# Differential attention's projection blocks as fp32 matmuls straight from the ring, with a scaled copy of the input made on GpSimd, and two weight splits moved ahead of a VectorE wait

## The chip, the core and the metric

The kernel runs on one core of a Trainium2 chip. TensorE (PE) does the matmuls, VectorE (DVE), ScalarE (ACT) and GpSimd (POOL) the elementwise work, and SyncE's queue (SP) issues most of the DMAs. The metric is the time of one execution in microseconds (us) on the device; lower is better.

## The reference

A trunk of two layers over 256 tokens of width 1024, all in fp32. Each layer projects the normalised input, mixes with two parallel groups of heads (an RWKV-7 recurrence, and differential attention), then does cross-attention and a feed-forward part (dense in layer 0, top-2 of 8 experts in layer 1). Cut to the part that the change touches:

```python
for l in range(DEPTH):
    h = rms_norm(x, mix_norm[l])                       # x / rms(x) * gain
    w_in = in_proj[l] if l == 0 else concat([in_proj[l], vres_down[l - 1]])
    proj = h @ w_in                                    # 1792 + 1536 (+ 32) columns
    p_rwkv = token_shift(proj[..., :RWKV_COLS], shift_mu[l])   # p + (prev - p) * mu
    p_diff = proj[..., RWKV_COLS:IN_COLS]              # q, k, v of differential attention
    y_rwkv, v_l = rwkv7_time_mix(p_rwkv, ...)
    y_diff = diff_attention(p_diff, ...)
    x = x + concat([y_rwkv, y_diff]) @ out_proj[l]
    ...
```

## The kernel before

The 256 tokens are two tiles of 128 (`t`), the width is eight tiles of 128 (`k`). Weights come from memory in blocks of 512 KB (two `k` by 512 columns), into a ring of four slots (`ring`), fetched by SP in the order of the list `blocks`.

**Most blocks are split.** TensorE multiplies in the format fp32r. To keep the accuracy of fp32 each weight block is split into a high part, made by ScalarE (`hi_of`, L405 where a gain is multiplied in), and the rest, made by VectorE (`lo_of`, L419: `ring*gain - w_hi`, two instructions of 128x512 for a block). The input is split the same way into `h_hi` and `h_lo`. `product` (L465, L466, L467) then takes three matmuls for each pair of tiles. There are three slots for split blocks (`NS`). A ring slot is given free by VectorE's half of the split, a split slot by TensorE's use.

**Some blocks are direct.** The cross-attention's `wkv` blocks are multiplied in fp32 straight from the ring (L530, the stationary operand is `mem_T`); such a matmul stands in the trace as two records. TensorE's use gives the ring slot free.

**The input projection** of a layer has 28 blocks of which the first 16 are for the recurrence, four blocks to a group of columns: keys (blocks 0 to 3), the low-rank columns (4 to 7, half as wide), receptance (8 to 11), values (12 to 15). Blocks 16 to 27 (`inb`, generator `rest`) are the 1536 columns of differential attention. Block numbers below count from the layer's first. The rms scale is applied when a result is evacuated; the gain `mix_norm` is in the split weights. ScalarE evacuates a group (L1257), GpSimd issues three DMAs that shift it by one token (`shift_in`, L1184 to L1186), and VectorE mixes (`mix`: a subtraction, a product with `mu`, a sum).

**Order.** Each engine has one program written out by hand. VectorE calls `split_to(n)` between its steps to do all splits up to block n. It starts the keys' mix (`next(k_mix)`, which waits for the shifted key columns) after block 7, and does blocks 8, 9 and 10 between the steps of the mixes. From the mixed keys it makes `NB[KK]` (L1683); ScalarE squares them (L1287), VectorE sums (L1541) and scales. TensorE's order is: the 16 first blocks with small products between them, the cumulative sums (L629), four blocks of `rest`, a small product (L639), four blocks of `rest`, the transposes of `aT`, `rT`, `bT`, `kT` (L489; they wait for VectorE's `elem`), and then the recurrence, between whose steps stand the last four blocks of `rest`, some cut into halves (one half for each `t`).

**GpSimd** in layer 1 alone forms the sum of `h_hi` and `h_lo` into `hT` (L1208, four instructions of 128x512), for a small product with `vresd_w` (32 columns), whose gain VectorE multiplies into the weights.

## Time and profile before

| | |
|---|---|
| median of 3 runs | 1944.86 us (the lowest is 1944.83; one run of 10261.35 stands beside them) |
| the profiled execution | 1950.51 us, of which the span of the core is 1948.7 us |
| mean granted TensorE clock | 0.972 |
| busy share of the span | PE 94%, DVE 78%, ACT 62%, POOL 3% |
| layer 0's input projection and recurrence | about 0 to 250 us of the span |
| layer 1's | about 555 to 810 us |
| the experts | about 940 us to the end |

The page's busy shares are means over stages that differ. The matmuls are pipelined and their ends modelled, so the spacing of their starts tells more than their durations. A row of a timeline has the start, the busy time, the engine, the line, the operation with its output and inputs, and in brackets how long the engine stood idle before it and what ended that. The granted clock is a share of full speed, and has two levels (1.2 and 2.4 GHz).

### The profile page before, as it was taken

How to read it: one execution, taken by the hardware profiler on the slowest of the kernel's cores; microseconds unless marked ns; L12 is line 12 of the kernel's file. 1: busy time of each engine (PE TensorE's matmuls, PEld its weight loads, DVE VectorE, ACT ScalarE, POOL GpSimd, SP SyncE). 2: the span in 40 equal slices, each digit the busy share in tenths (PEclk: the TensorE clock that was granted, in tenths of full speed). 3: DMA queues.
4: the chain of work that ended last, by engine and by line, in shares of the span. 5: the costliest groups of instructions: out<-in, count | busy, mean ns of one | idle time of the engine just before them, and what ended most of it. 6: DMA issues, size and time to landing. Idle time of an engine off the chain costs nothing.

```text
span 1948.7 us, 31880 instructions
## 1 busy us (share of the span) xinstructions
PE 1832.7 (94%) x10685; PEld 1452.9 (75%) x10685; DVE 1523.9 (78%) x2106; ACT 1198.5 (62%) x1616; POOL 54.1 (3%) x90
## 2 busy tenths in 40 slices
PE   6988898999999887998899999999999999999998
PEld 5665566788876665577788888888888888888886
DVE  5874666655568765674799999999999999999997
ACT  4632444555555312552677888778877878878785
POOL 2000000000020000000300000000000000000000
PEclk9999899999999897999899999999999999999999
DMA  8521163466654311451799999999999999999994
GB/s 255 177 89 56 55 211 98 150 188 187 190 165 142 119 45 34 132 170 61 280 372 341 359 379 336 358 359 345 379 337 361 356 352 370 338 366 347 358 371 152
DMA packets 224014, 474.54 MB, mean 244 GB/s; under 512 B 16680, under 2 KB 41400, under 8 KB 223376
## 3 DMA queue, kind: packets, MB, share of 16 engines
q1 hardware_dynamic: 219456, 458.29, 66.8%
q0 software_dynamic: 3472, 13.65, 2.2%
q8 instruction: 56, 0.92, 0.2%
q10 hardware_dynamic: 960, 1.10, 0.2%
q14 instruction: 70, 0.57, 0.1%
HBM read 468.25 MB, written 1.05 MB: 241 GB/s over the span
## 4 chain that ended last, share of the span: by engine, by line
PE 82%; DVE 11%; ACT 3%; DMA 2%; issue 2%; POOL 0%; DVEq 0%; ACTq 0%; POOLq 0%
PE psum L465 22%; PE psum L467 22%; PE psum L466 22%; PE psum L530 4%; PE psum L489 3%; DVE w_lo L419 2%; PE psum L1002 2%; PE psum L1049 1%; DMA SH<-proj 1%; DVE SH L1561 1%; PE psum L893 1%; DVE NB L1532 1%; DVE st L1538 1%; ACT hN L1261 1%; DVE SH L1532 1%
## 5 line engine op out<-in xcount | busy, mean ns | idle before, releaser
L465 PE MATMUL psum<-w_hi,h_hi 128*128 128x512 f32 (+1 forms) x1648 | 653.7, 397 | 31.5 <-DVE w_lo L419 29.5
L467 PE MATMUL psum<-w_hi,h_lo 128*128 128x512 f32 (+1 forms) x1648 | 644.3, 391 | 0.0
L466 PE MATMUL psum<-w_lo,h_hi 128*128 128x512 f32 (+1 forms) x1648 | 644.0, 391 | 0.0
L465 PEld LDWEIGHTS psum<-w_hi,h_hi 128*128 128x128 f32 x1648 | 312.6, 190 | 106.1 <-DVE w_lo L419 27.0
L467 PEld LDWEIGHTS psum<-w_hi,h_lo 128*128 128x128 f32 x1648 | 312.3, 189 | 66.5
L466 PEld LDWEIGHTS psum<-w_lo,h_hi 128*128 128x128 f32 x1648 | 312.9, 190 | 62.7 <-issue 0.5
L419 DVE SCALAR_TENSOR_TENSOR w_lo<-ring,col,w_hi 128x512 fp32r<-128x512 f32 (+1 forms) x232 | 163.4, 750 | 75.2 <-ACT w_hi L405 73.6
L405 ACT ACTIVATE w_hi<-ring,col 128x512 fp32r<-128x512 f32 (+1 forms) x232 | 150.6, 701 | 114.3 <-PE psum L467 109.6
L435 DVE TENSOR_TENSOR w_lo<-ring,w_hi 128x1024 fp32r<-128x1024 f32 x144 | 172.2, 1220 | 7.7 <-ACT w_hi L431 3.2
L431 ACT ACTIVATE w_hi<-ring 128x1024 fp32r<-128x1024 f32 x144 | 151.9, 1060 | 41.1 <-PE psum L467 41.1
L435 DVE TENSOR_TENSOR w_lo<-dproj,w_hi 128x1024 fp32r<-128x1024 f32 x120 | 145.8, 1222 | 17.1 <-ACT w_hi L431 13.0
L431 ACT ACTIVATE w_hi<-dproj 128x1024 fp32r<-128x1024 f32 x120 | 127.8, 1065 | 36.1 <-PE psum L467 36.1
L435 DVE TENSOR_TENSOR w_lo<-SH,w_hi 128x1024 fp32r<-128x1024 f32 x120 | 143.8, 1220 | 6.3 <-ACT w_hi L431 4.1
L431 ACT ACTIVATE w_hi<-SH 128x1024 fp32r<-128x1024 f32 x120 | 127.7, 1064 | 23.3 <-PE psum L467 22.9
L465 PE MATMUL psum<-h_hi 128*128 128x512 f32 x336 | 137.1, 408 | 0.1
L467 PE MATMUL psum<-h_hi,h_lo 128*128 128x512 f32 x336 | 131.6, 392 | 0.0
L466 PE MATMUL psum<-h_lo,h_hi 128*128 128x512 f32 x336 | 131.1, 390 | 0.0
L530 PE MATMUL psum<-ring,mem_T 128*128 128x512 f32 x256 | 123.0, 622 | 0.0
L435 DVE TENSOR_TENSOR w_lo<-proj,w_hi 128x1024 fp32r<-128x1024 f32 x96 | 115.2, 1220 | 6.9 <-ACT w_hi L431 5.1
L414 DVE TENSOR_TENSOR w_lo<-ring,w_hi 128x1024 fp32r<-128x1024 f32 x54 | 65.7, 1224 | 68.6 <-ACT w_hi L400 68.5
L400 ACT ACTIVATE w_hi<-ring 128x1024 fp32r<-128x1024 f32 x54 | 57.2, 1060 | 93.0 <-PE psum L467 78.4
L431 ACT ACTIVATE w_hi<-proj 128x1024 fp32r<-128x1024 f32 x96 | 101.3, 1064 | 19.0 <-PE psum L467 19.0
(315 smaller groups left out, 2336.0 us busy)
## 6 DMA issues: line engine op xcount, KB each, us to landing
ring<-in_expert_w_gu SPq DMA_DIRECT2D x128, 512.0 KB, 5.4
SH<-in_expert_w_gu SPq DMA_DIRECT2D x120, 512.0 KB, 5.8
proj<-in_expert_w_gu SPq DMA_DIRECT2D x104, 512.0 KB, 6.1
dproj<-in_expert_w_gu SPq DMA_DIRECT2D x72, 512.0 KB, 5.8
dproj<-in_expert_w_down SPq DMA_DIRECT2D x72, 512.0 KB, 5.0
ring<-in_expert_w_down SPq DMA_DIRECT2D x64, 512.0 KB, 5.1
ring<-in_in_proj SPq DMA_DIRECT2D x48, 512.0 KB, 4.4
ring<-in_dense_w_gu SPq DMA_DIRECT2D x88, 256.0 KB, 3.1
```

What stands on the lines that cost most here:

```text
L400: ins = act.activation(w_hi[:, i % NS, :], ring[:, n % RING, :], ACT.Copy)
L405: ins = act.activation(hi[:, k, :], src[:, k, :], ACT.Copy, scale=col[:, l, a + k:a + k + 1])
L414: ins = dve.tensor_tensor(w_lo[:, i % NS, :], ring[:, n % RING, :], w_hi[:, i % NS, :].bitcast(F32), SUB)
L419: ins = dve.scalar_tensor_tensor(lo[:, k, :], src[:, k, :], col[:, l, a + k:a + k + 1], hi[:, k, :].bitcast(F32), MUL, SUB)
L431: act.activation(hi_e[j % NS_E], ring_e[j % RING_E], ACT.Copy).then_inc(hi_done, 1)
L435: dve.tensor_tensor(lo_e[j % NS_E], ring_e[j % RING_E], hi_e[j % NS_E].bitcast(F32), SUB).then_inc(lo_done, 1)
L465: pe.matmul(o, h[0], w[0], start=start, stop=False, skip_group_check=True)
L466: pe.matmul(o, h[0], w[1], start=False, stop=False, skip_group_check=True)
L467: return pe.matmul(o, h[1], w[0], start=False, stop=stop, skip_group_check=True)
L489: last = pe.transpose(bank[0:m, i * P:i * P + n], s, ident[0:n, 0:n])
L530: last = pe.matmul(banks[c][t][:, 0:cw], memT[:, kb + k, t * P:(t + 1) * P], wd[:, k, :], start=(kb + k == 0), stop=(kb + k == 7), skip_gr ...
L1002: last = pe.matmul(bank[:, k * P:(k + 1) * P], hNv[:, t, (4 * g + k) * P:(4 * g + k + 1) * P], Psel[:, t, :], start=(t == 0), stop=(t == 1))
```

## The change

1. The 12 `inb` blocks of each layer become direct: no split, and TensorE multiplies in fp32 from the ring.
2. A direct block has no gain in it, so GpSimd makes the input with the gain, `xg = (h_hi + h_lo) * gain`, in two new buffers (`gained_x`): twelve instructions for a layer, six sums and six products, each product waiting for its sum. Eight of the twelve are 128x256, four 128x512. In layer 1 they stand where the four sums stood; in layer 0, where there was nothing, between the issue of the low-rank columns' shift and that of the receptance columns.
3. TensorE waits for them (`raw_ready`) ahead of `rest`. The small product with `vresd_w` uses the new buffers too, and VectorE's product of `vresd_w` with the gain goes.
4. VectorE does the splits of blocks 8 and 9 ahead of its wait for the shifted keys, 10 and 11 between the steps of the keys' mix; ScalarE does its half of block 11 ahead of the squares.

```diff
+        xg_b = nc.alloc_sbuf_tensor_at("xg_b", [P, 512], F32, offset=h_base + 4 * 2048)
+        xg_a = sb("xg_a", [P, 1536])
...
-            blocks += square_blocks(in_proj[l], chunks_in[0:4], gain=(l, COL["mix"])) + square_blocks(in_proj[l], chunks_in[4:], gain=(l, COL["mix"]))
+            blocks += square_blocks(in_proj[l], chunks_in[0:4], gain=(l, COL["mix"]))
+            blocks += [("direct", src, cw, None) for _, src, cw, _ in square_blocks(in_proj[l], chunks_in[4:])]
...
-                            if src[0] == "mT":
-                                last = pe.matmul(banks[c][t][:, 0:cw], memT[:, kb + k, t * P:(t + 1) * P], wd[:, k, :],
+                            if straight:
+                                lhs = memT[:, kb + k, t * P:(t + 1) * P] if src[0] == "mT" else x_gained(kb + k, t)
+                                last = pe.matmul(banks[c][t][:, 0:cw], lhs, wd[:, k, :],
                                                  start=(kb + k == 0), stop=(kb + k == 7), skip_group_check=True)
...
-                    pe.wait_ge(raw_ready, 4)
-                    pe.wait_ge(side_ready, 1)
+                    pe.wait_ge(raw_ready, 2 * 8)
+                    pe.wait_ge(lw_in, 80)
...
-                            last = pe.matmul(bank[:, 0:VR], hTv[:, k, t * P:(t + 1) * P], vresd_w[:, k, :], start=(k == 0), stop=(k == 7))
+                            last = pe.matmul(bank[:, 0:VR], x_gained(k, t), vresd_w[:, k, :], start=(k == 0), stop=(k == 7))
...
+                pe.wait_ge(raw_ready, 8 * (l + 1))
                 some(rest, 4)
...
+            def gained_x(l):
+
+                gain = col[:, l, COL["mix"]:COL["mix"] + KD]
+                if l == 0:
+                    pool.wait_ge(col_in, 16)
+                n = 8 * l
+                for g in range(2):
+                    for t in range(TT):
+                        B.wait_evacuated(pool, ("hT", l, 0, t, g))
+                        for k0, kn in ((0, 4),) if g == 0 else ((4, 2), (6, 2)):
+                            to = xgs[k0 // 6][:, k0 % 6:k0 % 6 + kn, t * P:(t + 1) * P]
+                            of = [m[:, k0 * SEQ:(k0 + kn) * SEQ].rearrange("p (k t) -> p k t", t=SEQ)[:, :, t * P:(t + 1) * P] for m in (h_hi, h_lo)]
+                            step(pool.tensor_tensor(to, of[0].bitcast(F32), of[1].bitcast(F32), ADD))
+                            n += 1 if kn == 2 else 2
+                            pool.tensor_tensor(to, to, bc(gain[:, k0:k0 + kn].unsqueeze(2), kn, P), MUL).then_inc(raw_ready, 1 if kn == 2 else 2)
+                pool.wait_ge(raw_ready, n)
...
                 if l:
-                    for g in range(2):
-                        for t in range(TT):
-                            B.wait_evacuated(pool, ("hT", l, 0, t, g))
-                            pool.tensor_tensor(part(hT, g, t), part(h_hi, g, t).bitcast(F32), part(h_lo, g, t).bitcast(F32), ADD).then_inc(raw_ready, 1)
+                    gained_x(l)
...
                 shift_in(l, LORA_)
+                if l == 0:
+                    gained_x(l)
...
-                        split_to(base + 11)
+                        split_to(base + 12)
...
-                    tt(vresd_w[:, :, :], vresd_w[:, :, :], bc(gains(l, "mix").unsqueeze(2), KD, VR), MUL)
...
+                split_to(base + 10)
                 next(k_mix)
-                split_to(base + 9)
+                split_to(base + 11)
                 next(k_mix)
-                split_to(base + 10)
+                split_to(base + 12)
                 for m in [lora_mix] + ([vr_mix] if l else []):
                     next(m)
                     next(m)
-                split_to(base + 11)
```

VectorE in layer 0 before the change, from the keys' mix to the squares' sum: `SH` holds the shifted columns and `hN` is `mu`, `shifted_in0` is the keys' shift, `weights_hi` ScalarE's half of a split.

```order
L1532 TENSOR_TENSOR SH<-SH,proj 128x2x512 [waits shifted_in0,mu_in]
L419 SCALAR_TENSOR_TENSOR w_lo<-ring,col,w_hi 128x512 [waits weights_hi,dve_step]
L419 SCALAR_TENSOR_TENSOR w_lo<-ring,col,w_hi 128x512
L1532 TENSOR_TENSOR SH<-SH,hN 128x2x512
L1667 TENSOR_TENSOR proj<-proj,SH 128x2x512 [waits dve_step]
L419 SCALAR_TENSOR_TENSOR w_lo<-ring,col,w_hi 128x512 [waits weights_hi,dve_step]
L419 SCALAR_TENSOR_TENSOR w_lo<-ring,col,w_hi 128x512
```

The same place on VectorE after the change:

```order
L426 SCALAR_TENSOR_TENSOR w_lo<-ring,col,w_hi 128x512 [waits weights_hi,mu_in]
L426 SCALAR_TENSOR_TENSOR w_lo<-ring,col,w_hi 128x512
L426 SCALAR_TENSOR_TENSOR w_lo<-ring,col,w_hi 128x512 [waits weights_hi]
L426 SCALAR_TENSOR_TENSOR w_lo<-ring,col,w_hi 128x512
L1558 TENSOR_TENSOR SH<-SH,proj 128x2x512 [waits shifted_in0]
L426 SCALAR_TENSOR_TENSOR w_lo<-ring,col,w_hi 128x512 [waits weights_hi,dve_step]
L426 SCALAR_TENSOR_TENSOR w_lo<-ring,col,w_hi 128x512
L1558 TENSOR_TENSOR SH<-SH,hN 128x2x512
L1692 TENSOR_TENSOR proj<-proj,SH 128x2x512 [waits dve_step]
L426 SCALAR_TENSOR_TENSOR w_lo<-ring,col,w_hi 128x512 [waits weights_hi,dve_step]
L426 SCALAR_TENSOR_TENSOR w_lo<-ring,col,w_hi 128x512
```

Two splits (blocks 8 and 9) now stand ahead of the wait for `shifted_in0`, and each later one is two blocks further on, so that the split of block 11 no longer stands behind the squares.

GpSimd in layer 0 after the change, from the last DMA of the low-rank columns' shift on (before, the rows L1186 and L1184 followed each other here):

```order
L1196 DMA SH<-proj 1x16x16
L1210 ISA
L1210 TENSOR_TENSOR xg_a<-h_hi,h_lo 128x4x128 [waits psum_evacuated4,columns_in]
L1212 TENSOR_TENSOR xg_a<-xg_a,col 128x4x128 [waits pool_step]
L1210 TENSOR_TENSOR xg_a<-h_hi,h_lo 128x4x128 [waits psum_evacuated5]
L1212 TENSOR_TENSOR xg_a<-xg_a,col 128x4x128 [waits pool_step]
L1210 TENSOR_TENSOR xg_a<-h_hi,h_lo 128x2x128 [waits psum_evacuated6]
L1212 TENSOR_TENSOR xg_a<-xg_a,col 128x2x128 [waits pool_step]
```

Six more rows of 128x2x128 follow before the receptance columns' shift (L1194).

TensorE in layer 0 before the change, at the start of `rest`: the first of eight blocks, of twelve matmuls each, of which six are shown.

```order
L465 MATMUL psum<-w_hi,h_hi 128x512 [waits weights_lo,psum_evacuated1,psum_evacuated0]
L466 MATMUL psum<-w_lo,h_hi 128x512
L467 MATMUL psum<-w_hi,h_lo 128x512
L465 MATMUL psum<-w_hi,h_hi 128x512
L466 MATMUL psum<-w_lo,h_hi 128x512
L467 MATMUL psum<-w_hi,h_lo 128x512
```

The same place after it, four whole blocks of four matmuls:

```order
L539 MATMUL psum<-ring,xg_a 128x512 [waits psum_evacuated1,block_in0,psum_evacuated0,raw_xT_ready]
L539 MATMUL psum<-ring,xg_a 128x512 x3
L539 MATMUL psum<-ring,xg_a 128x512 [waits block_in1]
L539 MATMUL psum<-ring,xg_a 128x512 x3
L539 MATMUL psum<-ring,xg_a 128x512 [waits block_in2]
L539 MATMUL psum<-ring,xg_a 128x512 x3
L539 MATMUL psum<-ring,xg_b 128x512 [waits block_in3]
L539 MATMUL psum<-ring,xg_b 128x512 x3
```

The wait for VectorE's split (`weights_lo`) is gone there; the block's arrival (`block_in`) and GpSimd's buffers (`raw_xT_ready`) are waited for.

## Rows read from the trace of the kernel before

**Rows 1.** The page, part 4: the whole span's chain, by engine.

```profile
PE 82%; DVE 11%; ACT 3%; DMA 2%; issue 2%; POOL 0%; DVEq 0%; ACTq 0%; POOLq 0%
```

**Rows 2.** Layer 0, VectorE's timeline: start us, us, engine, line, operation, [idle before <-releaser].

```profile
34.11 1.23 DVE L1532 TENSOR_TENSOR SH<-SH,proj 128x1024 f32<-128x1024 f32 x1 [6.26 <-DMA SH<-proj]
...
43.28 1.41 DVE L419 SCALAR_TENSOR_TENSOR w_lo<-ring,col,w_hi 128x512 fp32r<-128x512 f32 x2
44.61 1.22 DVE L1683 TENSOR_TENSOR NB<-proj,vec 128x1024 f32<-128x1024 f32 x1
48.18 1.41 DVE L419 SCALAR_TENSOR_TENSOR w_lo<-ring,col,w_hi 128x512 fp32r<-128x512 f32 x2 [2.35 <-ACT w_hi L405]
49.51 1.21 DVE L1541 TENSOR_REDUCE st<-NB 128x16 f32<-128x1024 f32 x1
50.76 1.42 DVE L419 SCALAR_TENSOR_TENSOR w_lo<-ring,col,w_hi 128x512 fp32r<-128x512 f32 x2
```

**Rows 3.** Layer 0, timelines of ScalarE and then TensorE, same columns.

```profile
45.86 1.06 ACT L1287 ACTIVATE NB<-NB 128x1024 f32<-128x1024 f32 x1 [10.56 <-DVE NB L1683]
46.83 3.77 ACT L405 ACTIVATE w_hi<-ring,col 128x512 fp32r<-128x512 f32 x6
...
36.93 0.77 PE L465 MATMUL psum<-w_hi,h_hi 128*128 128x512 f32 x1 [6.69 <-DVE w_lo L419]
```

**Rows 4.** GpSimd's timeline, layer 0: issue of the receptance columns' shift.

```profile
54.00 0.68 POOL L1184 DMA_DIRECT2D SH<-proj  x1 [18.84 <-ACT proj L1257]
```

**Rows 5.** Layer 1: GpSimd's sums, VectorE's splits 558 to 569 us; ns, min/median/max.

```profile
L1208 POOL TENSOR_TENSOR hT<-h_hi,h_lo x4: 1252/1268/1737, 560.4 to 566.7; 128x512 f32<-128x512 f32 x4
...
L419 DVE SCALAR_TENSOR_TENSOR w_lo<-ring,col,w_hi x6: 739/1070/4067, 558.7 to 567.2; 128x512 fp32r<-128x512 f32 x6
```

**Rows 6.** GpSimd's timeline in the experts' part: small operations.

```profile
945.27 1.10 POOL L1238 TENSOR_TENSOR NB<-NB 128x4 f32<-128x4 f32 x1
...
950.20 0.19 POOL L1241 TENSOR_TENSOR NB<-NB 128x1 f32<-128x1 f32 x1
```

**Rows 7.** VectorE's timeline there.

```profile
945.09 1.22 DVE L435 TENSOR_TENSOR w_lo<-ring,w_hi 128x1024 fp32r<-128x1024 f32 x1 [0.24 <-DVE hT L2118]
...
949.66 1.27 DVE L2136 TENSOR_TENSOR y_lo<-psum,y_hi 128x512 fp32r<-128x512 f32 x2
```

**Rows 8.** The chain of waits, an fp32 block and half block: start, us.

```profile
712.96 3.44 PE psum L530 x8
...
731.28 1.91 PE psum L530 x4
```

**Rows 9.** TensorE by stretch: us, busy (x), granted clock, DMA share, GB/s.

```profile
75.29:86.28 10.99, 10.99 (x51) 1.00 0.49 146
87.98:100.39 12.41, 11.46 (x51) 1.00 0.53 159
624.24:635.55 11.31, 11.31 (x50) 1.00 0.59 177
637.25:656.08 18.83, 14.34 (x51) 0.82 0.55 163
667.00:672.00 5.00, 5.00 (x42) 0.73 0.00 0
```

**Rows 10.** VectorE's timeline, layer 0: first and last of four splits.

```profile
79.89 1.41 DVE L419 SCALAR_TENSOR_TENSOR w_lo<-ring,col,w_hi 128x512 fp32r<-128x512 f32 x2
...
93.19 1.41 DVE L419 SCALAR_TENSOR_TENSOR w_lo<-ring,col,w_hi 128x512 fp32r<-128x512 f32 x2
```

**Rows 11.** Layer 1, timelines of TensorE and VectorE: waits behind splits.

```profile
650.79 0.79 PE L465 MATMUL psum<-w_hi,h_hi 128*128 128x512 f32 x1 [3.57 <-DVE w_lo L419]
...
673.62 0.75 DVE L419 SCALAR_TENSOR_TENSOR w_lo<-ring,col,w_hi 128x512 fp32r<-128x512 f32 x1 [0.68 <-ACT w_hi L405]
```

**Rows 12.** Layer 1, VectorE, then ScalarE: after the row scale, and key columns.

```profile
571.23 1.67 DVE L419 SCALAR_TENSOR_TENSOR w_lo<-ring,col,w_hi 128x256 fp32r<-128x256 f32 x4
...
573.55 0.69 ACT L1257 ACTIVATE proj<-psum,st 128x512 f32<-128x512 f32 x1 [0.61 <-PE psum L467]
```

More of the change, by code:

```diff
@@ L219, in decoder_trunk, with x_gained @@
         memT = mem_T[:, :].rearrange("p (k t) -> p k t", k=KD)
+        xgs = [m[:, :].rearrange("p (k t) -> p k t", t=SEQ) for m in (xg_a, xg_b)]
+        def x_gained(k, t):
+            return xgs[k // 6][:, k % 6, t * P:(t + 1) * P]
         mu = hN[:, 0:NMU]
@@ L520, in project_steps @@
                             nproj[0] += 1
-                    if src[0] == "mT":
+                    straight = src[0] == "mT" or name[0] == "inb"
+                    if straight:
                         wd = take_direct(cw)
```

2 lines of the change are left out of this document (1 added, 1 removed).

## The prediction

> **What bounds the kernel now.** I read the page's chain first, then the chain of waits in time for the two stretches that hold the input projection and the recurrence, then the timelines of VectorE, ScalarE, GpSimd and TensorE there. The chain is TensorE's for most of the span [rows 1], and over half of the span is the experts' loop, whose instructions the change leaves as they are. So only the two layers' stretches can move, and there three things take turns.
>
> From the shift of the keys to the low-rank products the chain is VectorE's and ScalarE's. In layer 0 VectorE waits for the shifted keys until 34.11 and then works nearly without a gap to the scaled keys at 44.61. The split of block 10 stands ahead of them (43.28), and that of block 11 (48.18, after 2.35 us idle) ahead of the squares' sum at 49.51 [rows 2]: ScalarE makes its half of block 11 only after the squares of 45.86 [rows 3]. TensorE waits 6.69 us for the split of block 8, which stands behind the shifted keys [rows 3], but that wait does not end last.
>
> The second thing is `rest`. In layer 0 the first eight blocks take TensorE from 75.29 to 100.39, back to back but for a small product and 0.95 us; the clock is full. In layer 1 they take from 624.24 to 656.08 [rows 9], with a wait of 3.57 us for a split and then half the clock (0.82 over that stretch) [rows 9, 11]: there VectorE binds.
>
> The third is the recurrence, where the last four blocks fill TensorE between short steps.
>
> **A block in fp32 against a split block.** Four split blocks take 10.99 us at full clock [rows 9], 2.75 for one. A direct block of the same shape takes 3.44, and its half 1.91 with the start [rows 8]. That is +0.69 for a block, +8.3 for the twelve of a layer, wherever TensorE is what ends last. VectorE is relieved of 12 x 1.41 = 16.9 us and ScalarE of 12 x 1.26 = 15.1 in each layer [rows 2, 3]; this counts only where they end last.
>
> *Layer 0, `rest`:* eight blocks now 8 x 3.44 = 27.5, and the small product between the two fours, 86.28 to 87.98, 1.7: 29.2 in place of 25.1 [rows 9], **+4.1**. VectorE's inputs to the next step do not bind: its last split ended at 94.6, and four of them (79.89 to 93.19) go [rows 10], so it is ready 5.6 us earlier, some 15 us before TensorE gets there.
>
> *Layer 1, `rest`:* 29.2 in place of 31.84 [rows 9], **-2.6**, since the wait and the half clock after it go.
>
> *The last four blocks, in the recurrence:* 4 x 0.69 = 2.8 if TensorE bound all through, nothing if the waits for the other engines cover it. In layer 0 I take **+1.5**, the middle, since the first of them already hides ScalarE's copies. In layer 1 the clock is 0.73 from 667 to 672 [rows 9], so one block takes about 4.1, and a pair of split instructions behind 0.68 us of waiting (673.62) stands on the chain [rows 11]; these go, up to 2.2. I take **-0.7**, between -2.2 and +2.8.
>
> The blocks' arrival adds no wait that I can find: a slot is now freed by TensorE's use, but four blocks lie ready when `rest` begins, and the DMA share is about a half there [rows 9].
>
> **The moved splits.** In layer 0, left alone, the scaled keys come 1.3 us earlier (block 10's split is no longer between) and end at 44.5; the squares follow at once, 1.06, and the sum starts at about 45.8 in place of 49.51 [rows 2, 3]: **-3.7** for all that follows (block 12's split, the scale, block 13, the low-rank products, the values and their shift). In layer 1 I take **-2.4**: VectorE then meets block 10 sooner than ScalarE's half of it is made, one such half (1.26) [rows 3]. Neither end can be on the plus side here, since no instruction is added.
>
> **The buffers made by GpSimd.** This is the term that decides. A sum of 128x512 takes 1.25 [rows 5], a tiny operation 0.19 [rows 6], so one of 128x256 about 0.72 (estimate, midway). The product with a stretched gain has no row; its nearest is the sum, and I take the same. Four of 1.25 and eight of 0.72 make 10.8 us for a layer. In layer 0 GpSimd stands idle from 35.16 to 54.00, 18.84 us [rows 4], so its own queue has room: the receptance shift behind it is late only if that work stretches past 54.
>
> But does VectorE go on meanwhile? In layer 1 now, four sums run between 560.4 and 568.3, and the splits of VectorE, 0.74 us at best, have a median of 1.07 and one of 4.07 [rows 5]. In the experts' part a GpSimd operation on four elements takes 1.10 beside a split that reads two tiles from SBUF, and 0.19 beside VectorE's operations that read PSUM [rows 6, 7]. So the two engines shut each other out for whole instructions. The Trainium skill says the same in "SBUF — State Buffer", section "SBUF: two separate sides": the shared port pair is an exclusive lock for the whole instruction, taken by a VectorE operation with two SBUF inputs only against a GpSimd one that reads SBUF. By that rule it speaks against this change, and the trace agrees.
>
> *Layer 0:* from 35.2 VectorE has ten instructions with two SBUF inputs up to the scaled keys (blocks 10 and 11, two of the keys' mix, three of the low-rank mix, the scaled keys). If the engines take turns, ten GpSimd instructions get between, 4 x 1.25 + 6 x 0.72 = 9.3, less 0.6 us of slack where VectorE waits for the low-rank shift: the keys end at about 53.2 in place of 44.5, **+8.7**. The bounds are 0 (VectorE isn't held) and 10.8 (all is lost). GpSimd ends at about 54.6, when its DMA would be due at 55 anyway.
>
> *Layer 1:* four sums stood there and cost already. Now the splits of block 3 end 1.2 later, and then the row scale, of whose twelve small steps nine have two inputs, meets the remaining five instructions of 128x256: 5 x 0.72 = 3.6. The row scale ended at 571.2 and will at about 576. The evacuation of the second key tile stood at 573.55, behind TensorE and not the row scale [rows 12], so 2 to 3 us of that shows; the splits of the low-rank blocks (571.23) move by the full 4.8, of which TensorE's own work covers 1.3. I take **+3.5**, between 0 and 4.8.
>
> The product of `vresd_w` that goes (about 0.4) stands in that shadow and counts nothing.
>
> **Sum.** Layer 0: -3.7 + 8.7 + 4.1 + 1.5 = +10.6. Layer 1: -2.4 + 3.5 - 2.6 - 0.7 = -2.2. Together **+8.4 us**. The sum is made on the profiled execution (1950.5, 5.6 above the median, of which nothing lies in these terms); on the median, 1944.9 + 8.4 = **1953**.
>
> **Rivals.** *(B) VectorE isn't held in layer 0*, because GpSimd finds gaps or yields: for it speaks that the tiny operations of the experts' part did not lengthen the splits beside them (1.22, as alone) [rows 7]; against it the splits of 0.74 that took 1.07 and 4.07 [rows 5]. Then layer 0 gives -3.7 + 5.6 = +1.9 and layer 1 -2.4 - 3.3 = -5.7: -3.8, **1941**, the other side of no change. It decides from the point where the two terms of holding, 12.2 together, fall under 3.8.
>
> *(C) GpSimd costs more than its sums say*: the products with the stretched gain take twice as long (+5.4 in a layer), or VectorE is held through several at a time, as it was for 4.07 us [rows 5]. With +5.4 in each layer the receptance shift is late too: +8.4 + 10.8 = +19, **1964**.
>
> *(D) The clock falls in layer 0.* With the splits of 8 to 11 done early and that of block 12 late, TensorE stands idle for some 7 us at about 50, as it does now before 36.93 [rows 3]. If blocks 12 and 13 then run at half clock and it shows, at most 2 x 2.75: +5, **1958**.
>
> *(E) TensorE's extra is hidden*, since another engine ends last in `rest`: layer 0's 4.1 and 1.5 fall out, +2.8, 1948. Against it: TensorE has no gap of note there [rows 9].
>
> **How the numbers follow.** Forecast (1948 to 1960) 0.45, B 0.22, C 0.13, D 0.1, E 0.07, and 0.03 for what I do not see. The range that leaves two in ten out reaches from between B and no change to C: **1938 to 1966**. Two per cent, about what a measurement of this kernel can tell from no change, is 39 us; the four terms of either sign do not reach it in any case above. Faster by over 2% 0.01, within 0.97, slower 0.02.
>
> **What would show it.** In the profile after: L1210 and L1212 on GpSimd from about 35 to 54.6 with durations over 0.72 and 1.25 where VectorE is in between, VectorE's scaled keys (L1708) ending near 53 (B: near 45); blocks of `rest` at 3.44 without a wait, aT's transposes some 29.2 after the first of them in both layers; in layer 1 the row scale ending near 576. I would be wrong if L1708 keeps to 45, if a wait for a block's arrival stands in `rest`, or if the products with the gain take far more than the sums.

## The result, and the profile after

The changed kernel takes 1958.63 us, the median of 7 runs (1954.63 to 1960.46); the kernel before took 1947.48 in the same rounds. The ratio is 1.0050, with a 95% interval of 1.0038 to 1.0062: the change costs half of one per cent, and the forecast's 1953 was 5.6 us too low, inside its range. The base had moved too: the sum stood on a median of 1944.9 of three runs, and the kernel before is at 1947.5 to 1949.0 in every later set of rounds. Against its own base the forecast is +8.4, and the measured difference +9.7 (0.50% of 1947.5, with 7.4 to 12.1 as its interval; the two medians lie 11.2 apart). The profiled execution has a span of 1956.3 us, against 1948.7.

The chain by engine, from the page of after:

```profile
PE 85%; DVE 10%; ACT 2%; DMA 2%; issue 2%; DVEq 0%; ACTq 0%
```

TensorE's share went from 82% to 85% [rows 1] and VectorE's and ScalarE's fell: that part of the change does what it says. VectorE's timeline of after in layer 0, which answers to [rows 2] (start us, us, engine, line, operation, count, idle before and who ended it):

```profile
35.19 1.22 DVE L1558 TENSOR_TENSOR SH<-SH,proj 128x1024 f32<-128x1024 f32 x1
38.57 3.23 DVE L426 SCALAR_TENSOR_TENSOR w_lo<-ring,col,w_hi 128x512 fp32r<-128x512 f32 x2 [2.16 <-ACT w_hi L412]
41.72 2.06 DVE L1558 TENSOR_TENSOR SH<-SH,hN 128x1024 f32<-128x1024 f32 x1
...
50.71 1.75 DVE L1708 TENSOR_TENSOR NB<-proj,vec 128x1024 f32<-128x1024 f32 x1
53.58 1.22 DVE L1567 TENSOR_REDUCE st<-NB 128x16 f32<-128x1024 f32 x1 [1.12 <-ACT NB L1313]
54.87 1.41 DVE L426 SCALAR_TENSOR_TENSOR w_lo<-ring,col,w_hi 128x512 fp32r<-128x512 f32 x2
```

GpSimd's timeline beside it, which answers to [rows 4]:

```profile
37.09 1.32 POOL L1210 TENSOR_TENSOR xg_a<-h_hi,h_lo 128x512 f32<-128x512 f32 x1
38.55 1.04 POOL L1212 TENSOR_TENSOR xg_a<-xg_a,col 128x512 f32<-128x512 f32 x1
39.54 1.71 POOL L1210 TENSOR_TENSOR xg_a<-h_hi,h_lo 128x512 f32<-128x512 f32 x1
...
44.45 1.48 POOL L1212 TENSOR_TENSOR xg_a<-xg_a,col 128x256 f32<-128x256 f32 x1
...
57.78 0.71 POOL L1194 DMA_DIRECT2D SH<-proj  x1 [4.85 <-ACT proj L1283]
```

A pair of splits that took 1.41 takes 3.23, the keys' product 2.06 in place of 1.22. The scaled keys end at 52.46 (45.83 before), GpSimd at 52.93; the wait of 2.35 us ahead of the squares' sum is gone, and yet the sum starts at 53.58 in place of 49.51.

TensorE's stretches of after, which answer to [rows 9], and the first layer's blocks in the chain of waits, which answer to [rows 8]:

```profile
78.48:107.81 29.33, 29.33 (x82) 13.98 (x82) 14.52 (x19) 3.54 (x8) 0.74 (x1) 1.00 0.53 167
635.66:664.92 29.26, 29.26 (x82) 13.90 (x81) 16.81 (x18) 4.15 (x9) 0.73 (x1) 1.00 0.57 173
```

```profile
78.60 13.85 PE psum L539 x32
...
109.72 3.44 PE psum L539 x8
```

Eight fp32 blocks and the small product take 29.3 us in both layers, back to back, at the full clock of 2.4 GHz (granted 1.00); before it was 25.1 and 31.8. Ahead of them, in layer 0, the clock is lower than it was. TensorE waits for a split (timeline), and the stretch from 57 to 63 us then has 0.57 as its granted clock (1.00 before):

```profile
56.44 0.76 PE L472 MATMUL psum<-w_hi,h_hi 128*128 128x512 f32 x1 [4.94 <-DVE w_lo L426]
```

```profile
57.00:63.00 6.00, 6.00 (x17) 4.47 (x16) 5.54 (x14) 4.69 (x9) 2.36 (x4) 0.57 0.78 219
```

Layer 1 has what the forecast had not seen. VectorE's timeline there, then ScalarE's:

```profile
564.66 6.59 DVE L426 SCALAR_TENSOR_TENSOR w_lo<-ring,col,w_hi 128x512 fp32r<-128x512 f32 x4
...
574.33 1.39 DVE L1561 TENSOR_SCALAR st<-st 128x2 f32<-128x2 f32 x3
...
589.09 1.41 DVE L426 SCALAR_TENSOR_TENSOR w_lo<-ring,col,w_hi 128x512 fp32r<-128x512 f32 x2 [4.79 <-ACT w_hi L412]
592.92 1.42 DVE L426 SCALAR_TENSOR_TENSOR w_lo<-ring,col,w_hi 128x512 fp32r<-128x512 f32 x2 [2.41 <-ACT w_hi L412]
594.25 1.22 DVE L1558 TENSOR_TENSOR SH<-SH,proj 128x1024 f32<-128x1024 f32 x1
```

```profile
587.66 1.33 ACT L412 ACTIVATE w_hi<-ring,col 128x512 fp32r<-128x512 f32 x2 [4.27 <-DMA ring<-in_in_proj]
591.55 1.33 ACT L412 ACTIVATE w_hi<-ring,col 128x512 fp32r<-128x512 f32 x2 [2.56 <-DMA ring<-in_in_proj]
```

and what the DMA queue of SyncE, which fetches the weights, waited for between 555 and 600 us (us in total, times, longest), with the same of before from 549 to 594 below it:

```profile
SPq L1143 <- DVE w_lo L426: 37.3, 11, 8.1
```

```profile
SPq L1133 <- DVE w_lo L419: 38.8, 11, 9.4
```

Four split instructions beside GpSimd's sums take 6.59 us (2.74 in act_gain_l1 below). But that is not new: before, the same four took 6.06 and the next two 3.08, which now take 2.05, and the queue waited as long for its slots. New are two things behind it. The row scale ends 14.4 us after the layer's start in place of 12.5, so the slots of blocks 8 and 9 come free 1.9 us later. And GpSimd issues the fetch of `mu` (912 KB) behind its twelve products, 14.1 us after the layer's start and not 9.6; GpSimd's timeline, before and then after:

```profile
568.34 0.56 POOL L1210 DMA_DIRECT2D hN<-in_mus  x1
```

```profile
578.78 0.58 POOL L1234 DMA_DIRECT2D hN<-in_mus  x1 [0.30 <-POOL xg_b L1212]
```

The weights of blocks 8 and 9 are issued right after it, at 580.03 and 580.82, and take 7.6 and 10.7 us to land, where they took 3.6 and 4.3. The second stands whole in the chain of waits:

```profile
580.82 10.71 DMA ring<-in_in_proj
```

ScalarE's halves wait 4.27 and 2.56 us for these weights, and VectorE's splits, which now stand ahead of the keys' mix, 4.79 and 2.41 for ScalarE. The mix starts at 594.25, 29.6 us after the layer's start, where it started 23.2 after it. In the four kernels that have the twelve products in layer 1 (after, no_reorder, pool_late, l1_old_order) the two fetches take 6.5 to 7.6 and 9.7 to 10.7 us; in the ten others, with `mu` issued 6.3 to 9.7 us after the layer's start, 3.6 to 4.0 and 4.3 to 6.7. No run moves the fetch of `mu` alone: that it is what slows the two is argued from these traces and not shown.

Where the kernels stand at a few events, from their timelines (us; layer 1's counted from its first GpSimd instruction, which is the third column; the last column is the first matmul of the experts' loop). Each is one trace. Where the code up to an event is the same, traces still differ: by 1.6 us at the aT transposes of layer 0 (reorder_alone and act_gain_split), and by 2.8 at those of layer 1 (pool_alone and pool_memset), so smaller differences in these columns can be chance:

| kernel | keys end, L0 | aT transposes, L0 | start of layer 1 | keys' mix, L1 | squares' sum, L1 | aT, L1 | experts |
|---|---|---|---|---|---|---|---|
| before | 45.8 | 100.4 | 558.7 | +23.2 | +38.6 | +97.4 | 937.9 |
| after | 52.5 | 107.8 | 564.7 | +29.6 | +41.9 | +100.2 | 944.7 |
| reorder_alone | 46.4 | 100.0 | 557.4 | +23.6 | +35.1 | +93.1 | 931.9 |
| no_reorder | 52.5 | 110.2 | 569.8 | +27.2 | +43.5 | +100.1 | 949.8 |
| pool_alone | 52.2 | 106.9 | 563.6 | +24.2 | +39.6 | +98.6 | 944.0 |
| pool_late | 48.4 | 108.2 | 565.0 | +29.5 | +41.8 | +100.1 | 944.9 |
| l1_old_order | 51.8 | 106.9 | 565.3 | +26.2 | +42.6 | +99.2 | 944.1 |
| act_gain_both | 45.9 | 102.6 | 562.3 | +22.7 | +34.2 | +90.8 | 934.2 |
| act_gain_l1 | 46.5 | 100.3 | 555.9 | +21.2 | +33.3 | +90.0 | 925.4 |
| vr_by_act | 47.0 | 101.5 | 558.4 | +21.5 | +36.8 | +94.9 | 931.1 |
| act_gain_split | 47.8 | 101.6 | 557.0 | +21.0 | +35.3 | +95.1 | 933.4 |
| act_gain_l0 | 46.1 | 101.1 | 563.7 | +22.6 | +34.1 | +91.8 | 936.5 |

### The profile page after: what moved, and what is told of

Same layout as the page of the kernel before. It is cut to its first block, busy times and chain, and to the rows that moved or that the text cites. A ratio compares the mean times of both kernels' runs of the same rounds, so it can differ in the third digit from the quotient of the medians.

```text
span 1956.3 us, 31589 instructions
## 1 busy us (share of the span) xinstructions
PE 1841.4 (94%) x10589; PEld 1429.3 (73%) x10589; DVE 1498.7 (77%) x2057; ACT 1167.0 (60%) x1568; POOL 75.6 (4%) x110
## 4 chain that ended last, share of the span: by engine, by line
PE 85%; DVE 10%; ACT 2%; DMA 2%; issue 2%; DVEq 0%; ACTq 0%
PE psum L472 22%; PE psum L474 21%; PE psum L473 21%; PE psum L539 8%; PE psum L496 2%; PE psum L1012 2%; DVE w_lo L426 1%; PE psum L1059 1%; DMA ring<-in_in_proj 1%; DVE SH L1587 1%; PE psum L903 1%; DVE st L1564 1%; DVE NB L1558 0%; PE psum L1023 0%; PE psum L1024 0%
## 5 line engine op out<-in xcount | busy, mean ns | idle before, releaser
L472 PE MATMUL psum<-w_hi,h_hi 128*128 128x512 f32 (+1 forms) x1552 | 613.4, 395 | 31.8 <-DVE w_lo L426 26.5
L474 PE MATMUL psum<-w_hi,h_lo 128*128 128x512 f32 (+1 forms) x1552 | 606.4, 391 | 0.0
L473 PE MATMUL psum<-w_lo,h_hi 128*128 128x512 f32 (+1 forms) x1552 | 606.0, 390 | 0.0
L472 PEld LDWEIGHTS psum<-w_hi,h_hi 128*128 128x128 f32 x1552 | 294.6, 190 | 101.4 <-DVE w_lo L426 21.3
L474 PEld LDWEIGHTS psum<-w_hi,h_lo 128*128 128x128 f32 x1552 | 294.3, 190 | 62.3
L473 PEld LDWEIGHTS psum<-w_lo,h_hi 128*128 128x128 f32 x1552 | 295.0, 190 | 59.0 <-issue 0.2
L426 DVE SCALAR_TENSOR_TENSOR w_lo<-ring,col,w_hi 128x512 fp32r<-128x512 f32 (+1 forms) x184 | 131.7, 762 | 77.0 <-ACT w_hi L412 76.0
L412 ACT ACTIVATE w_hi<-ring,col 128x512 fp32r<-128x512 f32 (+1 forms) x184 | 118.7, 697 | 95.1 <-PE psum L474 76.9
L438 ACT ACTIVATE w_hi<-dproj 128x1024 fp32r<-128x1024 f32 x120 | 127.9, 1066 | 35.3 <-PE psum L474 35.3
L438 ACT ACTIVATE w_hi<-SH 128x1024 fp32r<-128x1024 f32 x120 | 127.6, 1064 | 23.2 <-PE psum L474 22.9
```

What stands on the lines that cost most here:

```text
L412: ins = act.activation(hi[:, k, :], src[:, k, :], ACT.Copy, scale=col[:, l, a + k:a + k + 1])
L426: ins = dve.scalar_tensor_tensor(lo[:, k, :], src[:, k, :], col[:, l, a + k:a + k + 1], hi[:, k, :].bitcast(F32), MUL, SUB)
L438: act.activation(hi_e[j % NS_E], ring_e[j % RING_E], ACT.Copy).then_inc(hi_done, 1)
L472: pe.matmul(o, h[0], w[0], start=start, stop=False, skip_group_check=True)
L473: pe.matmul(o, h[0], w[1], start=False, stop=False, skip_group_check=True)
L474: return pe.matmul(o, h[1], w[0], start=False, stop=stop, skip_group_check=True)
```

## The experiments

Each was timed in five rounds beside the kernel before (the last two in three). Medians, and ratios to the kernel before in the same rounds with their 95% interval (medians of different kernels can come from different sets of rounds; each ratio is to the kernel before in its own):

| kernel | us | ratio |
|---|---|---|
| after | 1958.63 | 1.0050 (1.0038 to 1.0062) |
| reorder_alone | 1942.59 | 0.9974 (0.9962 to 0.9986) |
| no_reorder | 1961.73 | 1.0070 (1.0053 to 1.0087) |
| pool_alone | 1955.67 | 1.0036 (1.0023 to 1.0049) |
| pool_late | 1958.95 | 1.0055 (1.0039 to 1.0071) |
| l1_old_order | 1958.29 | 1.0053 (1.0040 to 1.0066) |
| vr_by_act | 1947.35 | 0.9997 (0.9988 to 1.0006) |
| act_gain_split | 1941.67 | 0.9953 (0.9941 to 0.9966) |
| act_gain_l1 | 1939.87 | 0.9958 (0.9944 to 0.9971) |
| act_gain_l0 | 1949.40 | 0.9998 (0.9982 to 1.0015) |
| act_gain_both | 1947.42 | 0.9996 (0.9983 to 1.0009) |
| pool_one_input | 1948.74 | 1.0002 (0.9989 to 1.0015) |
| pool_memset | 1948.58 | 0.9998 (0.9986 to 1.0010) |

### The moved splits alone, and the change without them

reorder_alone is the kernel before with

```diff
+                split_to(base + 10)
                 next(k_mix)
-                split_to(base + 9)
+                split_to(base + 11)
                 next(k_mix)
-                split_to(base + 10)
+                split_to(base + 12)
...
-                split_to(base + 11)
```

and ScalarE's half of block 11 ahead of the squares; no_reorder is the changed kernel with this undone.

> The kernel before with only the splits moved (blocks 8 and 9 ahead of VectorE's wait for the shifted keys, 10 and 11 between the keys' steps, ScalarE's half of 11 ahead of the squares), in both layers; nothing on GpSimd, nothing in fp32. Theory A (my terms of -3.7 and -2.4): the move takes out waits and adds none; the squares' sum starts near 45.8 us in layer 0, and the whole is some 6 us faster (ratio 0.997). Rival B: the move makes VectorE wait for the arrival of blocks 8 and 9 ahead of the keys' mix, and block 12's transfer, released early, slows those in flight (in the changed kernel the transfers of 24 to 50 us took 9.5 us in the median in place of 5.3, and layer 1's keys' mix started at 594.3, 5 us after its columns can have landed): the keys' mix starts later by 1 us in layer 0 and by 4 to 6 in layer 1, and the whole is between 3 us faster and 3 us slower.

> The changed kernel with its splits put back where they stood before (the fp32 blocks and GpSimd's buffers stay). Theory A: 6 us slower than the changed kernel, so near +16 on the kernel before. Rival B: layer 1's keys' mix starts right when its columns land, and the whole is as fast as the changed kernel or up to 4 us faster, near +6 to +10 on the kernel before.

The moved splits gain: 5.1 us by the ratio alone, 3 to 4 within the change, where the theory had 6 for both and the rivals at most 3 alone and nothing within it. The rival's late keys' mix did not come in reorder_alone either (33.95 and +23.6 us, for 34.11 and +23.2 before). But the gain is not where the forecast put most of it. In layer 0 the squares' sum comes 2.0 earlier (47.55 for 49.51) and not 3.7: VectorE, now two blocks further on, waits 1.02 and 1.82 us for ScalarE's halves of blocks 10 and 11, and those 2.67 and 4.30 for their weights, so the keys end at 46.4, 0.6 later than before. The aT transposes come 0.4 earlier: VectorE waits the rest away behind TensorE's low-rank products (1.55 us of idle time before, 3.04 in reorder_alone):

```profile
61.26 1.42 DVE L1561 TENSOR_TENSOR NB<-psum,vec 128x512 f32<-128x512 f32 x2 [3.04 <-PE psum L615]
```

There the clock differs. From 57 to 63 us, first before and then in reorder_alone, where TensorE had just waited 2.25 us for a split:

```profile
57.00:63.00 6.00, 5.47 (x20) 3.07 (x22) 4.42 (x7) 3.12 (x5) 0.00 (x0) 1.00 0.86 264
```

```profile
57.00:63.00 6.00, 6.00 (x20) 3.04 (x18) 2.60 (x4) 2.26 (x4) 0.00 (x0) 0.84 0.95 323
```

What that costs can be read from act_gain_l0 and act_gain_both below, whose code is the same in layer 0. One has 1.00 in this stretch and the other 0.79, and the low-rank products reach VectorE 12.2 and 13.8 us after the start of the squares' sum; before it is 12.2, in reorder_alone 13.7. So the clock takes back some 1.5 of the 2.0 us.

In layer 1 4.3 us of gain stand at the aT transposes.

### GpSimd's work alone, and the same work later

pool_alone is the kernel before with GpSimd's twelve products of layer 0 (nobody reads them); pool_late is the changed kernel with

```diff
                 shift_in(l, LORA_)
-                if l == 0:
-                    gained_x(l)
...
                     pool.dma_start(vec[:, VEC_PARTS[1]], vecs[0, VEC_PARTS[1]].partition_broadcast(P)).then_inc(vec_in, 16)
+                    gained_x(l)
```

> The kernel before with GpSimd's twelve instructions of layer 0 added at their place of the changed kernel, and nothing that reads their result. It measures the disputed cost alone. Theory A (the two engines shut each other out for whole instructions): VectorE's instructions with two SBUF inputs from 35 to 53 us are stretched, the scaled keys (45.8 before) end 8 to 9 us later, and the whole is 8 to 9 us slower. Rival B (VectorE has slack there, so that most is hidden): under 4 us.

> The changed kernel with GpSimd's work of layer 0 moved behind the issue of the receptance columns' shift (about 55 us), where VectorE works on steps of 16 columns and on PSUM. Theory A: the scaled keys come 8 us earlier (near 45), the work then meets the receptance mix and some splits instead, of which part is hidden; the whole is 3 to 6 us faster than the changed kernel. Rival B: the same instructions are held up later for as long, and the whole stays within 2 us of the changed kernel.

Work that nobody reads, on an engine that stood idle, costs 7.0 us of the whole run, between the 8 to 9 of the theory and the under 4 of the rival; 6.3 stand at the scaled keys (52.2 for 45.8) and 6.5 at the aT transposes. VectorE's timeline of pool_alone shows them:

```profile
35.53 3.28 DVE L423 SCALAR_TENSOR_TENSOR w_lo<-ring,col,w_hi 128x512 fp32r<-128x512 f32 x2
38.73 2.29 DVE L1555 TENSOR_TENSOR SH<-SH,hN 128x1024 f32<-128x1024 f32 x1
```

Put behind the receptance shift (from 56 us) the same work lets the keys end 4.1 us earlier (the theory had 8: VectorE waits 2.55 and 0.70 us for the halves of blocks 10 and 11), and the run gains nothing, as the rival had it. VectorE is then held in the splits ahead of the low-rank products, which took 4.06 us before, and aT comes at 108.2 in place of 107.8:

```profile
56.10 8.59 DVE L426 SCALAR_TENSOR_TENSOR w_lo<-ring,col,w_hi 128x512 fp32r<-128x512 f32 x6
```

Neither of the two places tried is free.

### ScalarE makes the gained input

In these kernels ScalarE writes it, straight from the transposes in PSUM, and all of GpSimd's sums and products are gone (layer 1's four sums of the kernel before too):

```diff
+                        for i in range(4):
+                            a = COL["mix"] + 4 * g + i
+                            ins = act.activation(x_gained(4 * g + i, t), bank[:, i * P:(i + 1) * P], ACT.Copy, scale=col[:, l, a:a + 1])
```

act_gain_both has fp32 blocks in both layers, act_gain_l1 in layer 1 alone:

> The changed kernel with one difference: the gained fp32 input of both layers is written by ScalarE (16 activations of 128x128 from the transposes' PSUM banks with the gain as scale) and GpSimd's twelve products of both layers are gone; ScalarE does layer 0's behind block 11 and layer 1's behind the squares of the row scale. Theory (GpSimd's elementwise work, not the fp32 blocks, carries the loss): layer 0 keeps the fp32 blocks' price of +4.1 us less what the recurrence gave back, 1.6, and loses GpSimd's 6.3, so its net over the kernel before falls from +5.8 to about +1 to +3; layer 1 also loses the four sums of the kernel before, scaled keys 3 to 4 us earlier than with either kernel's GpSimd work; whole run 1937 to 1943 us, ratio 0.994 to 0.998. Rival (the fp32 blocks themselves carry the loss: PSUM banks, weights straight from the ring and the later transfers): the run stays within 3 us of the changed kernel, 1955 to 1960.

> As act_gain_both, but layer 0's last eight blocks of the in projection are split as in the kernel before, so that fp32 blocks and gained input stand in layer 1 alone (ScalarE writes the latter). Theory: layer 0 pays nothing, so this is 1 to 3 us faster than act_gain_both, 1935 to 1941 us. Rival (fp32 blocks in layer 0 cost nothing once VectorE is free, since their splits are gone from it): the same as act_gain_both within 1 us, or slower.

Sixteen copies take ScalarE 4 us, mostly in a gap of its own (VectorE waits 2.58 us for the half that stands behind them, at 566.82); the first ten, in act_gain_l1:

```profile
561.77 2.68 ACT L1284 ACTIVATE xg_a<-psum,col 128x128 f32<-128x128 f32 x10
```

With the fp32 blocks kept and GpSimd silent the change's loss is gone (1947.4 for 1958.6, 11 us; 7.7 when both are brought to the same clock as below, which leaves 2.4 over the kernel before), so GpSimd's arithmetic carries most of it. The run takes away a little more than the change added, though: the kernel before's four sums of layer 1, and 3.3 us of the time at which `mu` is fetched there. The blocks still eat what the moved splits earn, and the 1937 to 1943 expected of act_gain_both was missed by 4 us. act_gain_l1 came where it was expected (1935 to 1941), but further from act_gain_both than the 1 to 3 us of either text.

vr_by_act takes only layer 1's four sums from the kernel before, act_gain_split adds the moved splits to that, act_gain_l0 the fp32 blocks of layer 0 to that:

> The kernel before with one difference: layer 1's unsplit gained input, which the value residual's matmuls read, is written by ScalarE (16 activations) and not by GpSimd's four sums, and VectorE's product of the gain into the residual's weights is gone; all blocks split as before, no split moved. It measures what GpSimd's four sums of layer 1 cost the kernel before. Theory (they hold VectorE from 560 to 571 us): row scale of layer 1 ends 2 to 4 us sooner, whole run 1942 to 1946 us. Rival (VectorE was not on the path there; the blocks' arrival was): no change, 1947 to 1949 us.

> The kernel before with the moved splits of the change and layer 1's residual input written by ScalarE (vr_by_act plus reorder_alone): no GpSimd elementwise work, and no fp32 block of the in projection in either layer. With act_gain_l1 (fp32 in layer 1), act_gain_l0 (fp32 in layer 0) and act_gain_both it makes a two by two table of the fp32 blocks alone. Theory (fp32 blocks cost TensorE 4.2 us each layer and give back what VectorE and ScalarE no longer split): reorder's 5 us and vr_by_act's 1 add, 1941 to 1944 us, so act_gain_l1 (1939.9) is 1 to 4 us faster: layer 1's fp32 blocks gain a little. Rival (fp32 blocks cost the same in both layers, 7 us as between act_gain_both and act_gain_l1): this one is the fastest of the four, 1932 to 1935 us.

> As act_gain_split, but with layer 0's last eight blocks of the in projection in fp32 (ScalarE writes their gained input); layer 1 split. Theory (by the trace of act_gain_both the aT transposes of layer 0 come 2.2 us later with fp32 blocks; the rest of the 7.5 us between act_gain_both and act_gain_l1 is the clock in layer 0's recurrence and not the blocks): 1.5 to 3.5 us slower than act_gain_split, 1943 to 1947 us, aT transposes of layer 0 at 102 to 103 us. Rival (the whole 7.5 us belong to layer 0's fp32 blocks): 6 to 9 us slower than act_gain_split, 1948 to 1952 us.

vr_by_act: VectorE is set free, the row scale of layer 1 ends 8.4 us after the layer's start in place of 12.5, and the keys' mix then waits for the next thing:

```profile
579.88 1.22 DVE L1546 TENSOR_TENSOR SH<-SH,proj 128x1024 f32<-128x1024 f32 x1 [5.85 <-DMA SH<-proj]
```

It starts 1.7 earlier, and the run is 0.6 us faster by the ratio, with an interval on both sides of no change. The theory's 1942 to 1946 is missed: what the sums take from VectorE there, the shift's transfer takes next.

The fp32 blocks alone (in layer 0 together with ScalarE's copies), with no GpSimd work around them, make this table (medians in us; in brackets the mean of the runs, each brought to a mean granted clock of 0.976 with the slope of the last section, "at equal clock"):

| | layer 1 split | layer 1 fp32 |
|---|---|---|
| layer 0 split | 1941.7 (1942.5) | 1939.9 (1944.2) |
| layer 0 fp32 | 1949.4 (1948.4) | 1947.4 (1949.8) |

Layer 0's fp32 blocks cost 7.6 us by the medians, 7.4 and 8.8 by the ratios and 5.8 at equal clock, in both columns alike; layer 1's lie between -1.9 and +1.6 and can't be told from nothing. The slope was found within kernels. Whether a kernel's own mean clock is chance or its doing is not known, so both figures stand. So of act_gain_l0's two texts the rival was right in the total.

Where layer 0's cost lies the traces tell only in part. act_gain_both's aT transposes come 2.2 us after act_gain_l1's; act_gain_l0's come at 101.1, 0.5 before act_gain_split's, which began its keys' mix 1.0 later, and 1.4 before act_gain_both's, by the clock from 57 to 63 us alone. The last four blocks are clearer. From the aT transposes to the first transposes of `proj` behind those blocks it is 24.8 us with split blocks and 26.5 with fp32 ones where the first 25 us are granted 1.00, and 26.4 and 28.1 where they are granted 0.93: 1.6 to 1.7 at either clock. From there on the length varies by more than what is sought: the recurrence takes 161.7 us in before and 157.9 in pool_one_input, with the same code.

### Layer 1 with the old order

```diff
-                split_to(base + 10)
+                split_to(base + (8 if l else 10))
                 next(k_mix)
-                split_to(base + 11)
+                split_to(base + (9 if l else 11))
                 next(k_mix)
-                split_to(base + 12)
+                split_to(base + (10 if l else 12))
...
+                if l:
+                    split_to(base + 11)
```

> The changed kernel with one difference: in layer 1 the splits stand as in the kernel before (keys' first step, block 9's half, keys' second step, block 10's half, low-rank mixes, block 11's half); layer 0 keeps the moved splits. Theory (the keys' mix of layer 1 waits because the halves of blocks 8 and 9, ahead of it now, wait for their weights to land): the keys' mix starts 2 to 3 us earlier than with the changed kernel, at 591 to 592 us, but the splits' 3.7 us come back behind it, so that the squares' sum is at 606 to 608 us and the run within 2 us of the changed kernel, 1957 to 1961. Rival (the late arrival is caused by GpSimd's longer work alone and the order has no part): the keys' mix stays at 594 us and the run is 3 to 4 us slower, since the moved splits gained that much in layer 1 of the kernel before.

The keys' mix starts at 26.2 after the layer's start and not at 29.6, so the new wait is the order's; the sum is at 42.6 for 41.9 and the run is the same within its interval. ScalarE's halves wait for their weights here as well (3.17 and 2.67 us), so what makes the weights late is not the order. Here too `mu` is fetched 14.1 us after the layer's start, the two fetches take 6.5 and 9.7 us, and the shift for which the mix waits takes 8.3 (3.9 before). In layer 1 the moved splits are worth 4.3 us at the aT transposes without GpSimd's products (reorder_alone) and nothing with them (no_reorder +100.1, after +100.2); within the change their 3 us come from layer 0 (107.8 for 110.2).

### What holds VectorE

> pool_alone (the kernel before with GpSimd's twelve products of layer 0, read by nobody), but each product reads one SBUF operand: a tensor_scalar by 2.0 of the high part, then one in place, same shapes, same order. In pool_alone VectorE's two products of 128x512 at 35.5 us take 3.28 us (1.41 without GpSimd), its 128x1024 product 2.29 (1.22), and the scaled keys end at 52.2 us (45.8 before). Theory (VectorE's operations with two SBUF inputs are held for as long as a GpSimd operation reads SBUF, however many inputs it reads): the stretches scale with GpSimd's busy time, keys end 3 to 7 us late (49 to 53 us), run 1952 to 1956. Rival (only a GpSimd operation with two inputs holds VectorE): VectorE's durations stay at 1.41 and 1.22, keys end at 46 to 47 us, run 1947 to 1950.

> As pool_one_input, but the twelve operations are memsets of the same tiles, which read nothing and only write. Theory (the hold is on reading: the Trainium skill's page on SBUF counts GpSimd operations that read it): VectorE's durations stay at 1.41 and 1.22, scaled keys end at 45.8 to 47 us, run 1947 to 1950. Rival (a write holds as well): VectorE's 128x512 pair takes over 2 us beside them and the keys end 2 us or more late.

Both are pool_alone with other operations in the same places. VectorE's timeline of pool_one_input, then GpSimd's:

```profile
34.77 2.02 DVE L423 SCALAR_TENSOR_TENSOR w_lo<-ring,col,w_hi 128x512 fp32r<-128x512 f32 x2
36.71 1.21 DVE L1555 TENSOR_TENSOR SH<-SH,hN 128x1024 f32<-128x1024 f32 x1
37.95 1.52 DVE L1690 TENSOR_TENSOR proj<-proj,SH 128x1024 f32<-128x1024 f32 x1
```

```profile
35.31 1.83 POOL L1204 TENSOR_SCALAR xg_a<-h_hi 128x512 f32<-128x512 f32 x1
37.29 1.98 POOL L1206 TENSOR_SCALAR xg_a<-xg_a 128x512 f32<-128x512 f32 x1 [0.15 <-POOL xg_a L1204]
...
48.11 0.85 POOL L1206 TENSOR_SCALAR xg_a<-xg_a 128x256 f32<-128x256 f32 x1
```

and the same of pool_memset:

```profile
36.47 1.42 DVE L423 SCALAR_TENSOR_TENSOR w_lo<-ring,col,w_hi 128x512 fp32r<-128x512 f32 x2
37.80 1.22 DVE L1555 TENSOR_TENSOR SH<-SH,hN 128x1024 f32<-128x1024 f32 x1
```

```profile
37.42 0.56 POOL L1204 MEMSET xg_a<- 128x512 f32 x1
```

Memsets do not hold VectorE in the 4.8 us that they last. Reads of one operand keep GpSimd busy as long as the two-operand work did (15.9 us from 35.3 to 51.2, for 15.6 in pool_alone), but stretch VectorE by little: 2.02 where pool_alone has 3.28, 1.21 where it has 2.29. From the start of the keys' mix to the scaled keys' end it is 13.0 us, against 17.9 in pool_alone and 11.7 before, and the run is as long as before. GpSimd gives way too: its 128x256 operations take 0.84 and 0.85 us while VectorE stands idle (46.5 to 48.9 us), and up to 1.39 beside it; those of 128x512 take 1.52 to 1.98. The operation changed together with its number of operands (a tensor_scalar for a tensor_tensor), so which of the two matters is not separated. The rival's keys (46.5) and time came true, its unchanged durations did not; the theory, that any read of SBUF holds VectorE for as long as the GpSimd operation runs, falls. For pool_memset the theory held (keys at 47.5 after a mix that began 1.1 us later than before).

## Why the forecast was right, and where it was off

**Blocks in fp32, `rest`.** Right to a tenth: 29.3 in both layers for 29.2, full clock, no wait for an arriving block. +4.2 in layer 0, -2.6 in layer 1, as a duration. In layer 1 the -2.6 hangs on the clock of the trace of before: split blocks take 31.8 us there, 31.0 to 32.1 in the six other traces that have them with a lower clock in part of the stretch, and 29.1 in act_gain_l0, where 1.00 is granted throughout. What was not seen is that VectorE, which has the first of these splits ahead of the receptance's mix, reaches that mix 1.9 earlier without them (64.5 in act_gain_both, 66.4 in act_gain_l1), so that `rest` starts earlier and, in this pair, 2.2 of the 4.2 are left at the aT transposes.

**The last four blocks.** +1.6 at 25 us into the recurrence for a forecast of +1.5 in layer 0. In layer 1 it is -0.5 for -0.7, and that agreement is luck: before has a granted clock of 0.93 and 0.94 in that stretch (27.0 us) and after 1.00 (26.5), while six other traces with split blocks, granted 0.99 or 1.00, take 25.4 to 25.5. Against those fp32 costs 1.0 in layer 1 too. Later in the recurrence after even gained on before (layer 0: 160.0 us from aT to the next vectors' fetch, 161.7 before), and that is the clock, not the change. The stretches 80 to 120 us behind the aT transposes, of before and then of after (length, busy time of PE, PEld, DVE, ACT and POOL, then the granted clock, the DMA share and GB/s):

```profile
180.39:200.39 20.00, 13.91 (x298) 10.55 (x299) 9.93 (x24) 3.72 (x9) 0.00 (x0) 0.79 0.11 35
200.39:220.39 20.00, 17.63 (x189) 12.09 (x185) 15.34 (x41) 6.84 (x18) 0.00 (x0) 0.87 0.10 30
```

```profile
187.81:207.81 20.00, 14.46 (x338) 10.97 (x335) 10.04 (x25) 4.22 (x9) 0.00 (x0) 0.83 0.13 42
207.81:227.81 20.00, 14.92 (x176) 9.56 (x174) 16.81 (x47) 7.77 (x23) 0.00 (x0) 1.00 0.17 54
```

**The moved splits in layer 0.** Wrong size and wrong place: -3.7 was read at the squares' sum, where 2.0 came, and carried to the end; at the aT transposes 0.4 was left. The keys were to end at 44.5 and end at 46.4 in reorder_alone, since the moved splits meet weights that have not landed, a wait the forecast put at nothing. And "for all that follows" was not held against the low-rank products, for which VectorE waits next, at a lower clock.

**The moved splits in layer 1.** -4.3 alone (forecast -2.4), but nothing within the change, because of the wait below.

**GpSimd holding VectorE in layer 0.** It was the term that decides, and right in kind: VectorE is held where it was said to be. "The two engines shut each other out for whole instructions" is too strong. Whole turns would cost 9.3 us, and in pool_alone VectorE's instructions are stretched by 6.9. In those 15.6 us GpSimd's twelve operations get done, 9.9 us at the shortest durations in these traces (1.25 and 1.04 for sum and product of 128x512, 0.72 and 0.61 for 128x256), and some 9.2 us of VectorE's at their durations of before, so about 3.5 us went side by side (an estimate from these rows). Forecast +8.7 at the keys; the term alone measures +6.3 there, +7.0 in the run (4.6 at equal clock). That the keys ended at 52.46, near the 53.2 foretold, is partly luck: from reorder_alone's 46.4 it is +6.0, and the forecast started 1.9 too early. Rival B, VectorE not held, is refuted by pool_alone, and C by GpSimd's end at 52.9 (54.6 foretold): the product with the stretched gain takes no longer than the sum.

**GpSimd in layer 1.** +3.5 was too little at first and for another reason. The row scale ended 14.4 us after the layer's start for 12.5 (+1.9, forecast +4.8); the step that failed is the one after it, "the blocks' arrival adds no wait that I can find". It was looked for in `rest`, where there is none, and not at blocks 8 and 9. In layer 0 the forecast asked which DMA stands behind GpSimd's work; in layer 1, where the fetch of `mu` does, it did not ask. The wait for the two blocks moved the keys' mix by 6.4 us and left +3.4 at the sum and +2.9 at the aT transposes, `rest`'s -2.6 included.

**The sum.** By experiments of their own: moved splits -5.1, GpSimd in layer 0 +7.0, fp32 blocks in layer 0 +7.6, together +9.5, which leaves next to nothing (+0.2) for the rest of layer 1. The forecast had -6.1, +8.7, +5.6 and +0.2 in the same order: the moved splits' gain was put 1.0 too large and GpSimd's price 1.7 too large, the fp32 blocks' 2.0 too small, so some of the total's agreement is cancellation. The parts do not simply add, either: within the change the moved splits are worth 3 to 4 us and not 5.1, which leaves -1 to -2 for the rest of layer 1. Why layer 0's fp32 blocks cost 5.8 to 7.6 us when the trace shows 2.2 at the aT transposes and 1.6 behind them stays open; each pair of profiled executions differs by the clock in the recurrence, by more than what is missing.

D (a colder clock in layer 0) came true as to the clock and not as to the price. TensorE waited 4.94 us and the granted clock was 0.57 from 57 to 63 us, but VectorE's wait for the low-rank products is 1.19 us, less than the 1.55 before, and they come 12.4 us after the start of the squares' sum for 12.2: the lower clock costs at most 1.2 us here and not 5. E (TensorE's extra hidden) is refuted: the blocks cost more than forecast, not nothing.

## What to carry to other kernels

An idle GpSimd is not free while VectorE is on the path with two SBUF operands: ask which instructions the two will share time with, and put a copy with a scale on ScalarE from PSUM instead, or leave the work out. And ask which DMAs the busy engine issues behind its new work, and what they will then be in flight beside: in layer 1 a fetch of 912 KB, issued 4.5 us later, stood beside the two fetches that VectorE waited for. Of the versions tried act_gain_split and act_gain_l1 beat the kernel before by 0.4 to 0.5% (7 to 9 us; 3 to 5 at equal clock), with the moved splits and the gain on ScalarE; neither needs fp32 blocks in layer 0.

## What the hardware did that was not expected

- **What GpSimd's operation reads decides how long VectorE is held.** With two operands, VectorE's pair of splits went from 1.41 to 3.28 us; with one (a tensor_scalar), to 2.02, and GpSimd was stretched as well; with none (memsets, 0.56 us for 128x512), 1.42. The Trainium skill, "SBUF — State Buffer", section "Who interferes with whom", has VectorE's operations with two SBUF inputs contend with any GpSimd instruction that reads SBUF and not with one that only writes it. The memsets agree (1.42 for 1.41); for one operand the runs show contention, but a fifth of the time lost at the scaled keys with two (1.3 of 6.2 us).
- **The mean granted clock tells much of the scatter.** Over 186 runs of all these kernels the time falls by 1.23 us for each 0.001 of mean granted clock within a kernel, and runs of one kernel differ by up to 15 us (act_gain_l0: 1940.9 to 1955.9). Differences under 3 us between two kernels can be the clock's.
